# A mixture-of-experts loop with pairs ordered by the address of the load, two loop variants, split gather and sums, and sixteen identity products ahead of the loop

## The reference, cut to what matters

```python
def hier_moe(h, wr_g, br_g, wr_e, br_e, w_gu, w_down):
    """Group router top-1, then expert router top-2 inside the chosen group; gate = p_group * renormalised p_expert."""
    ...
    pg, gi = lax.top_k(p_group, 1)
    ...
    pv, pi = lax.top_k(jax.nn.softmax(e_in, axis=-1), TOP_K)
    gates = pg * pv / jnp.sum(pv, axis=-1, keepdims=True)
    expert_id = gi * EXPERTS_PER_GROUP + pi
    return grouped_experts(xf, expert_id, gates, w_gu, w_down).reshape(B, S, D)

    def expert_block(args):
        xb, e = args
        a, b = jnp.split(xb @ w_gu[e], 2, axis=-1)
        return (jax.nn.silu(a) * b) @ w_down[e]
```

## Time and profile before

| | us |
|---|---|
| median of 3 runs | 2210.24 |
| lowest, highest | 2209.28, 2216.31 |
| the profiled execution | 2208.49 |
| its span, first to last instruction | 2206.7 |

### The profile page before, as it was taken

The page is one execution under the profiler, slowest core; times in us unless marked ns, Lnnn a source line. Parts: engine busy times, 40 slices in busy tenths (PEclk is TensorE's granted clock), DMA queues, the critical chain, the costliest instruction groups (busy, mean ns, idle before and its releaser), DMA issues.

```text
span 2206.7 us, 37943 instructions
## 1 busy us (share of the span) xinstructions
PE 2080.8 (94%) x15688; PEld 1519.7 (69%) x15689; DVE 884.1 (40%) x1459; ACT 687.7 (31%) x1070; POOL 80.3 (4%) x119
## 2 busy tenths in 40 slices
PE   7997899998999998889999999989998999999998
PEld 5876899988999898744544444588987444444454
DVE  5866677755643544521111111156366111111112
ACT  3434455253553456511111111144342111111111
POOL 0110111101000200000000000000000000000000
PEclk9998999999999999989999999989998999999999
DMA  9731388912654251689999999625642899999992
GB/s 360 266 128 39 118 306 320 333 42 77 249 190 175 78 189 39 255 330 422 421 422 422 421 422 422 267 90 189 214 189 98 366 421 421 422 422 422 422 422 123
DMA packets 108115, 603.25 MB, mean 273 GB/s; under 512 B 10078, under 2 KB 10532, under 8 KB 58868
## 3 DMA queue, kind: packets, MB, share of 16 engines
q1 hardware_dynamic: 95872, 559.39, 64.0%
q0 software_dynamic: 11872, 42.35, 5.2%
q10 hardware_dynamic: 276, 0.13, 0.0%
HBM read 600.74 MB, written 1.05 MB: 273 GB/s over the span
## 4 chain that ended last, share of the span: by engine, by line
PE 85%; DVE 5%; ACT 4%; DMA 3%; issue 3%; SPq 0%; DVEq 0%; ACTq 0%
PE bank L945 20%; PE bank L957 10%; PE bank L552 10%; PE bank L553 9%; PE bank L554 9%; PE bank L929 6%; PE bank L976 5%; PE bank L582 4%; DMA dense_w<-in_w_in 1%; PE bank L562 1%; PE bank L563 1%; PE bank L561 1%; PE bank L632 1%; DMA dense_w<-in_mlp_w 1%; ACT w_high L428 1%
## 5 line engine op out<-in xcount | busy, mean ns | idle before, releaser
L945 PE MATMUL bank<-expert_w,work 128*32 128x512 f32 (+1 forms) x4032 | 446.1, 593 | 19.1 <-issue 19.1
L945 PEld LDWEIGHTS bank<-expert_w,work 128*32 128x32 f32 (+1 forms) x4032 | 156.7, 110 | 307.0 <-issue 307.0
L435 DVE TENSOR_TENSOR w_low<-dense_w,w_high 128x2048 fp32r<-128x2048 f32 x112 | 256.1, 2290 | 223.5 <-ACT w_high L428 222.9
L428 ACT ACTIVATE w_high<-dense_w 128x2048 fp32r<-128x2048 f32 x120 | 228.6, 1911 | 313.4 <-DMA dense_w<-in_mlp_w 197.6
L957 PE MATMUL bank<-expert_w,work 128*32 128x512 f32 (+1 forms) x2016 | 226.4, 594 | 0.0
L2092 DVE TENSOR_TENSOR work<-work,bank 128x512 f32<-128x512 f32 x32 | 22.0, 688 | 391.4 <-ACT work L1419 391.4
L929 PEld LDWEIGHTS bank<-work 128*128 128x128 f32 x1088 | 137.3, 205 | 43.9 <-issue 43.9
L957 PEld LDWEIGHTS bank<-expert_w,work 128*32 128x32 f32 (+1 forms) x2016 | 63.6, 110 | 144.4 <-issue 144.4
L929 PE MATMUL bank<-work 128*128 128x128 f32 x1088 | 143.7, 293 | 13.9 <-issue 7.7
L552 PE MATMUL bank<-u_pairs_mlp,w_high 128*128 128x256 f32 x512 | 146.1, 285 | 7.3 <-ACT u_pairs_mlp L1144 5.9
L553 PE MATMUL bank<-u_pairs_mlp,w_low 128*128 128x256 f32 x512 | 145.6, 284 | 0.0
(11 more groups left out here) (387 smaller groups left out, 3610.3 us busy)
## 6 DMA issues: line engine op xcount, KB each, us to landing
expert_w<-in_expert_w_gu SPq DMA_DIRECT2D x256, 1024.0 KB, 13.5
expert_w<-in_expert_w_down SPq DMA_DIRECT2D x128, 1024.0 KB, 9.8
dense_w<-in_mlp_w SPq DMA_DIRECT2D x64, 1024.0 KB, 5.3
dense_w<-in_ret_w_in SPq DMA_DIRECT2D x24, 1024.0 KB, 5.3
u<-in_ada_w POOLq DMA_DIRECT2D x40, 512.0 KB, 6.0
work<-in_ada_w POOLq DMA_DIRECT2D x40, 512.0 KB, 7.0
dense_w<-in_fox_w_in SPq DMA_DIRECT2D x16, 1024.0 KB, 5.1
dense_w<-in_w_in SPq DMA_DIRECT2D x12, 1024.0 KB, 7.9
```

The source lines that it names most:

```text
L428: nc.scalar.activation(HIGH_OF[at], dense_w[:, at % RING], ACT.Copy, scale=scale).then_inc(S("w_high_ready"), 1)
L435: ins = nc.vector.tensor_tensor(w_low[:, at % RING], dense_w[:, at % RING], high, ALU.subtract)
L945: last = mm(free[half][cols, :], rows[:, k, cols], pieces[:, k // 2, a, k % 2, half * 512:(half + 1) * 512], start=k == 0, stop=k == KT - 1)
```

## The change

1. **The order of a pair.** If the second expert of a pair has more tokens than 64 and the pair fits as 96 + 32, the two experts change places: SyncE reads a number `swap` from `more_i` (now 64 numbers instead of 48) at the top of each turn of its loop and computes the address of the load from it. SyncE also waits for `more_known_{l}` ahead of its loop.
2. **Two variants** (64 + 64, and 96 + 32 as tiles of 64, 32 and 32 slots) instead of three. The 64 + 64 variant is used wherever both counts are at most 64.
3. **Split gather.** The normalized rows are kept as `hn_high` and `hn_low` in float32r, and `pick` is float32r: 32 products of 128 columns instead of 16 in float32. ScalarE makes all four parts of `hn_high`, VectorE the four of `hn_low`, two ahead of the router's logits and two behind the choice.
4. **Split sums.** `add_up` uses `y_high` and `y_low` times the 0/1 matrix `pickT`, 16 products of 256 columns in float32r instead of 8 in float32. The weight of each slot (`slot_w`) is taken by a reduction and multiplied in while the results leave the banks: ScalarE takes both halves, then VectorE both halves of the rest.
5. **Sixteen products with the identity** (`run_on`), 6 ahead of the counting products and 10 ahead of the first gather.
6. The numbers of slots are computed with other VectorE instructions, and GpSimd loads `ffn_gain` later.

The program of TensorE ahead of the first loop, before: the router (L886), `take_h` (L894), the counting products (L901 to L905), the first gather (L929).

The core of the diff:

```diff
-SHARES = (UNIT, 2 * UNIT, 3 * UNIT)
+SLOTS = P // 2
+LARGE = SLOTS + UNIT
...
+                    e = ds(2 * pair + a if swap is None else 2 * pair + swap if a == 0 else 2 * pair + 1 - swap, 1)
...
+                sp.wait_ge(S(f"more_known_{l}"), 1)
                 with sp.Fori(1, PAIRS) as i:
+                    swap = sp.value_load(more_i[0:1, ds(i + 3 * PAIRS, 1)], min_val=0, max_val=1)
...
+                def run_on(n):
+                    for _ in range(n):
+                        mm(free[0][:, 0:SEQ], ident, K("rope_cos"), start=True, stop=True)
...
-                            last = mm(free[2 + half][:, (k % 4) * P:(k % 4 + 1) * P], every_other(hn_tok[:, tt], k),
-                                      source[:, tt, :], start=tt == 0, stop=tt == TT - 1)
+                            for x in (hn_high, hn_low):
+                                last = mm(free[2 + half][:, (k % 4) * P:(k % 4 + 1) * P], x[:, tt, k * P:(k + 1) * P], source[:, tt, :],
+                                          start=tt == 0 and x is hn_high, stop=tt == TT - 1 and x is hn_low)
...
+                tiles_of = {SLOTS: [(slice(0, SLOTS), 0), (slice(SLOTS, P), 1)],
+                            LARGE: [(slice(0, SLOTS), 0), (slice(SLOTS, LARGE), 0), (slice(LARGE, P), 1)]}
...
-                        last = mm(total[k // 2][:, (k % 2) * SEQ:(k % 2 + 1) * SEQ], y_sb[:, k * P:(k + 1) * P],
-                                  pick_wT.rearrange("p t n -> p (t n)"), start=False, stop=False)
+                        for y in (y_high, y_low):
+                            last = mm(total[k // 2][:, (k % 2) * SEQ:(k % 2 + 1) * SEQ], y[:, k * P:(k + 1) * P], pickT,
+                                      start=False, stop=False)
...
-                    for first in SHARES:
+                    for first in (SLOTS, LARGE):
...
-                    fn(y_sb[:, 0:512], free[2][:, :], ACT.Copy).then_inc(done, 1)
+                    for half in range(2):
+                        fn(y_high[:, half * 512:(half + 1) * 512], free[2 + half][:, :], ACT.Copy, scale=slot_w).then_inc(done, 1)
...
-                    V.tensor_copy(pick_wT, free[1][:, 0:SEQ].rearrange("p (t n) -> p t n", t=TT)).then_inc(done, 1)
-                def take_y(done):
-                    V.tensor_copy(y_sb[:, 512:1024], free[3][:, :]).then_inc(done, 1)
+                    V.tensor_reduce(slot_w, free[1][:, 0:SEQ], AX.X, ALU.add)
+                    V.tensor_scalar(pickT, free[1][:, 0:SEQ], 0.0, None, ALU.is_gt).then_inc(done, 1)
+                def take_y(made, at, done):
+                    for half in range(2):
+                        dve.wait_ge(made, at + half + 1)
+                        eight = slice(half * 512, (half + 1) * 512)
+                        last = V.scalar_tensor_tensor(y_low[:, eight], free[2 + half][:, :], slot_w, y_high[:, eight].bitcast(f32),
+                                                      ALU.mult, ALU.subtract)
+                    last.then_inc(done, 1)
```

More of the change, by code:

```diff
@@ L250, in build @@
         flog = part(wk, 8704, 4, SEQ)[0:FOX_HEADS]
-        hn_tok = part(wk, 0, TT, D)
+        hn_high = parts("hn_high", "work", 0, [TT, D])
+        hn_low = parts("hn_low", "u", 0, [TT, D])
         xg = part(wk, 2048, KT, P)
@@ L2019, in experts @@
-                place, held = (rt[:, b:b + 4].rearrange("p (c t) -> p c t", c=2) for b in (26, 30))
-                def both(v):
-                    return v.unsqueeze(1).broadcast_to([P, 2, TT, E])
-                need, spare = share[:, 0, :], share[:, 1, :]
-                fit, first_units, more, upto = (share[:, b, :] for b in (2, 3, 4, 5))
-                units = iota[:, UNIT:P:UNIT].unsqueeze(1).broadcast_to([P, PAIRS, 3])
-                for a, test in ((0, ALU.is_gt), (1, ALU.is_le)):
-                    last = V.tensor_tensor(over[:, PAIRS * a:PAIRS * (a + 1), :], counts[:, a, :].unsqueeze(2).broadcast_to([P, PAIRS, 3]),
-                                           units, test)
@@ L2050, in experts @@
-                link(last)
+                pos = bank(t)[:, 0:TT * E].rearrange("p (t n) -> p t n", t=TT)
+                counts = e_sum.rearrange("p (i a) -> p a i", a=2)
+                crowd, few, turned, own, next_own, both_fit, large, swap, more, upto = (share[:, b, :] for b in range(10))
+                room_of, key_of = (room[:, b, :].rearrange("p (i a) -> p a i", a=2) for b in range(2))
+                link(V.tensor_copy(e_sum, bank(t)[:, 2 * E:3 * E]))
+                V.tensor_tensor(crowd, counts[:, 0, :], counts[:, 1, :], ALU.max)
```

156 lines of the change are left out of this document (83 added, 73 removed).

## The result

The changed kernel takes **2252.16 us** (median of 4 runs, 2249.38 to 2257.40), the kernel before 2209.76 in the runs beside it: a ratio of 1.0198, with a 95% interval of 1.0156 to 1.0239. I had forecast 2185, with a range of 2172 to 2204. It came out **slower by 42 us**, and the forecast of its direction was wrong.

What follows compares the result with a forecast made beforehand. TensorE ended each turn (29.54 us), with the loads close behind at 29.8 and soon setting the pace. Gains of 11.6, 12.1 and 0.6 us, together 24.3, took 2208.49 to 2184.2; forecast 2185, range 2172 to 2204.

Steps and rivals of the forecast that it cites:

- The variants: In project and down of the expert loops: tiles of 64, 32 and 32 cost the same as the existing ones, cost 0.
- Ahead of the loops: From choosing the experts to the first gather: about -1.8 us in the first layer and -1.4 in the second.
- after six identity products at full clock they take 1.1 less: First layer's counting products, at half clock before, would take 1.1 us less; with VectorE's later choice, +0.4 net.
- the sum: Whole kernel: gains of 11.6 us in the first loop, 12.1 in the second, 0.6 behind them, together 24.3, giving 2184.2.
- Split sums: add_up in each turn: sixteen float32r products take 1.92 us instead of 3.46, a gain of 1.54 a turn.
- Split gather: Gather in each turn: 32 float32r products at 0.120 us take 3.84 instead of 3.97, a gain of 0.13.
- The turn of TensorE: TensorE's own time per pair in the expert loops falls by 1.9 us to about 27.7.
- The loads end the turn: In the expert loops, loads at 422 GB/s keep a turn of 29.8 us and set the pace from about pair 7.
- pair 0's turn: First pair of each loop: its middle is 1.8 us shorter, so the stream of loads starts that much earlier.
- The clock while TensorE waits: Rival in the loops: the clock falls during waits for loads, giving 2188 to 2192; clock or prologue as before had 0.08.
- The rivals: Slow products 2272 (0.16), in between 2190 to 2212 (0.06), room 2148 (0.04), clock 2188 to 2192 (0.08), more 2172 to 2179 (0.06).
- The one that ended slower: Rival at the gather: small float32r products take 0.24 us each, a turn of 31.4, about 2272 us; chance 0.16.

Runs made afterwards that it cites:

- experiments 1 to 3: Changed kernel, mixed pairs in four tiles of 32: 2193.93 us; kernel before, first loop in tiles of 32, 32, 64: 2585.64; changed kernel, products ordered by size: 2250.68.
- experiment 1: Changed kernel with the 96 + 32 variant in four tiles of 32 slots instead of 64, 32 and 32: 2193.93 us, 0.9933 of before.
- Experiment 6: Changed kernel with four tiles of 32 and without the six identity products; sums back in float32: 2193.00 us, or instead the gather back in float32: 2180.61 us.
- experiment 7: Changed kernel with four tiles of 32, without the six identity products, loading half of each w_down piece from the second loop's second pair on: 2158.16 us.
- experiment 9: Changed kernel with four tiles of 32, eight identity products in a free bank, five before the gather, float32 gather and no hn_low: 2177.12 us, 0.9833 of before.
- experiment 4: Changed kernel with four tiles of 32, without the six identity products and their wait: 2184.36 us; without all sixteen: 2189.60 us.
- experiment 5: Changed kernel with four tiles of 32, eight identity products into an early free bank and five instead of ten ahead of the gather: 2180.17 us, 0.9873 of before.

## Why the prediction was wrong, step by step

- **The variants: this step failed.** I wrote that "64, 32 and 32, which the trace lacks and which lies between" should cost the same, and put 0. It doesn't lie between: four of 32 and two of 64 each are one size. The two sizes exclude each other: `project` took 31.78 us and `down` 15.95 instead of 13.9 and 7.1, and a mixed turn costs 26.9 us more. Three pairs of 32 made 58 us of difference (experiments 1 to 3). The step broke the rule that I followed for the gather: an operation that the trace doesn't show is bounded from both sides. One behind the other, twice the length of `project` and `down`, would have been my upper bound and a rival: 3 x 20.9 = 63 us, less about 22 that the loads would have taken anyway (80.7 - 58.4 in experiment 1), so 2185 + 41 = 2226. Even that is no upper bound: a mixed `project` took 31.78 us and not 2 x 13.9 = 27.8, for the changes between the sizes come on top.
- **Ahead of the loops: also wrong.** Forecast -1.8 and -1.4, measured +4.6 and +5.1 with the variants mended. The order of TensorE's instructions was right before me; what I left out is the wait that stands with the six, for a bank that VectorE frees behind the choice. Of the term "after six identity products at full clock they take 1.1 less" the counting is right: it ran at full clock (0.31 us for two records) in the changed kernel too. But the six did not: behind a wait of 4.25 us they ran at 0.51 of the clock and took 5.3 us. With the six and their wait gone it was +0.7 and +4.1 (some 3 of it a stop); only with eight in a free bank and five ahead of the gather -2.7 and -2.2. The choice came 0.8 us later, not 1.4. The gather gained what was forecast (3.9 us at full clock), but the half clock then fell on the first `project`, which lost 1.6 to 1.8, a price that the sum doesn't have.
- **Split sums: right.** 1.91 us against 1.92, a gain of 1.55.
- **Split gather: right in its size, wrong in its cause.** 3.72 against a forecast of 3.84; from its start to the next transposes 3.63, which is 0.113 us a product. Experiment 6 gives nearly all of the gain to the layout.
- **The turn of TensorE: 27.15, forecast 27.7.** Most of the difference is the two tiles in place of four, 0.41 us, which I had put at 0 as well. Pair 9 of the kernel before had it, but I read only the lengths of its products.
- **The loads end the turn: right.** 29.8 us at 422 GB/s, from pair 6 on (forecast: 7), and the landing of the expert loads grows and then stands still (experiment 7 shows the bound itself). In the changed kernel's second loop, the turns of pairs 2, 8 and 13:

```profile
DMA to landing us min/median/max: 10.4/13.6/18.5
...
DMA to landing us min/median/max: 18.4/23.1/25.4
...
DMA to landing us min/median/max: 18.3/23.1/25.3
```

  Experiment 1's loops are 13.2 and 9.8 us shorter than before; the sum without its part ahead of the loops had 9.8 and 10.7. The sum had pair 0's turn 1.8 us shorter in each. It was 6.6 shorter in the first loop, where the stop was gone, and 0.9 in the second, where one of 2.28 us stood ahead of the gather: put in, these give 14.6 and 9.8.
- **The clock while TensorE waits: the rival fell.** 1.00 throughout the turns with waits of 0.9 and 1.3 us. The section on HAM oscillation that I cited from the Trainium skill (TensorE: Matmul & The Clock Gate) describes longer waits than these. No turn with such waits started at half clock, but the first turn of each loop did, although TensorE had paused only 1.67 us before it in the first layer. It was so in every kernel with the split gather (15.3 to 16.3 us for the first `project`); behind a float32 gather and the same pause of 1.7 us it took 13.95 and the clock stood at 1.00 (experiment 9 in both layers, the old gather of experiment 6 in the first). So the pause alone doesn't do it, and the split gather has a price of 1.7 us a loop that the sum lacks. The loads can hide it: with the old gather the first loop took 463.96 us, against 463.99 in experiment 4.
- **The rivals.** None of mine was what happened. The one that ended slower had its mechanism at the gather, which runs at 0.113 us a product.

With the two failed steps mended (experiment 5), the kernel stands at 2180, where the sum said 2184.2. That is close in part by luck. From pair 1 to the last `down` the loops gained 7.4 and 6.5 us, where the sum had 8.0 and 8.9. Pair 0's turn gained 6.4 and 5.1, where it had 1.8: the sum left the stop of 4.04 us as it is, and in this kernel it is gone. And SyncE's eight issues take 8 x 0.333 = 2.7 us, not the 3.3 of the prediction, which changes nothing in the sum.

**What stays open.** A stop of some us stands near the first pair's branches and moves with the program: 4.04 us behind `project` in the earlier trace rows, 4.62 ahead of `project` in the changed kernel's second layer, none behind `project` in its first. In the records of the instructions it is one compare-and-branch of TensorE (3.3 us in the changed kernel, 6.1 in the kernel before) for which no engine is waited. I take it for the fetching of the program, which wasn't tested. The traces fit that: within each of the 18 such branches of over 2 us, in all the kernels here, a transfer of 16 KB on the DMA queue of kind `instruction` starts, 0.1 to 3.8 us behind the branch's start. But such transfers also run where nothing stops, so the cause stays argued. It makes up to 4 us a loop, and the versions above differ in it by chance.

## What to carry to other kernels

Before two shapes are put side by side, ask what the engine must have in common for both. "It lies between two rows of the trace" holds for a length, not for a mode. When an instruction is added to fill a pause, look at what it waits for before what it costs: here the filler waited for the very instruction that ended the pause. And where loads are 0.3 us a turn from being the bound, a gain in the turn is worth the slack that is left, here some 6 us a loop, and not its size times the number of turns.

## What the runs showed of the hardware that I had not expected

- Tiles of 32 and of 64 columns of TensorE don't run side by side: 1.98 us for a group of 64 + 32 + 32 by 512 float32 columns, 0.87 for 32 x 4 or 64 x 2; a change between the sizes costs about 0.13 us.
- float32r products of 128 columns take 0.113 us each (3.63 / 32), those of 256 start every 0.120. Two of them are hardly faster than one float32 product of 128 columns (2 records, 0.115 each), and much faster than one of 256 (2 records, 0.216 each).
- A float32 product of 128 columns whose weights are every other column took 0.121 us a record (3.87 / 32), one with its weights in a row 0.115 (3.67 / 32). The two stand in different kernels.
- Twice as many instructions for the same columns leave the products as long as they were, and cost 0.4 us where `down` passes over into the next `project`.
- The loads of this one core held 422 GB/s in the loops and no more; without a sixth of their bytes they run at 385 and TensorE doesn't wait.
- The granted clock fell to 0.50 at the first `project` of each loop, 1.67 us behind the gather in the first layer, in every kernel with the split gather, and not behind a float32 gather and the same pause where no stop stood ahead of it. From pair 1 to the last `down` it stayed at 1.00, with TensorE waiting 0.9 and 1.3 us a turn. Identity products that had to wait 4.25 us themselves ran at half clock.
